# Retention: where a head's decay logarithms and exponentials stand in the order of VectorE and ScalarE

## The chip, the cores and the metric

One core of a Trainium2 chip runs one program: two layers of a first block (retention, windowed attention, feed-forward) and one layer of a second block. The metric is the device time of one execution in microseconds; lower is better. The engines are TensorE (PE in the profile, its weight loads PEld), VectorE (DVE), ScalarE (ACT), GpSimd (POOL) and SyncE (SP). Each has its own instruction queue and works it off strictly in order; they meet only at semaphores.

## What is computed

The change touches only the retention branch of the two layers of the first block. There are 8 heads, head width 64 for q and k and 128 for v, over 528 positions (16 meta tokens and 512 others). The reference works in chunks:

```
decay_in = jnp.where(mask[None], jnp.exp(lg * jnp.maximum(rel, 0.0)[None]), 0.0)
s = jnp.einsum('bhncd,bhnkd->bhnck', q, k) * decay_in[:, None]
o_in = jnp.einsum('bhnck,bhnke->bhnce', s, v)
...
mu = jnp.mean(o, axis=-1, keepdims=True)
var = jnp.mean(jnp.square(o - mu), axis=-1, keepdims=True)
o = (o - mu) * lax.rsqrt(var + EPS)
return o * jax.nn.silu(gate)
```

with a forward direction and a backward one, each with its own decay per head. The kernel uses the closed form without chunks: for one head, out = (scores times decay) times v over all positions, where the decay of a pair of positions is the exponential of min(a·rel, b·rel), rel being their distance with its sign, a and b the two directions' logarithmic decays. Then comes a normalisation over the 128 columns of v, and the product with silu of the gate.

## The kernel before

The kernel is written by hand for each engine: for each stage a function for PE, ACT, DVE and POOL, whose Python loops print that engine's queue. Nothing reorders afterwards. `wait_ge` waits on a semaphore of another engine, `tick` names the event that an instruction signals.

The retention stage is `ret_pe`, `ret_act`, `ret_dve`, `ret_pool`, run once in each of the two layers (l = 0 and 1). In layer 0 a tile is 528 wide, in layer 1 it is 512 wide. All four loop over h = 0 to 9 and hold a software pipeline: a turn h works on the scores of head h, on the mean of head h-1 and on the variance, scale and gate of head h-2. A "turn" below is one such pass.

- PE, turn h: five score tiles, j = 0 to 4 (L192, inputs QK; tile 0 has 16 rows, the others 128, the contraction is over 64 rows); the gate projection of head h-2, called g below (L302 to L304); five products with v, called ret (L198), each of which needs its decayed score tile; the variance of h-2 and the mean of h-1 (L192, inputs WK, MH).
- DVE, turn h: two instructions that make the 128x928 table of logarithms DT[h % 2] (L623 and L625, "logs"); five multiplications of a score tile in PSUM by a window of the table (L635, "decay"); the low half of a coming weight tile (L270); the scaling of head h-2 (L643, "normed"); the subtraction of the mean of head h-1 (L647, "dev").
- ACT, turn h: the exponential of the table in place (L587, "decays"); the high half of a coming weight tile (L260); silu of g (L593); the copy of ret out of PSUM (L598, "o"); Ln and Exp that make the reciprocal deviation of head h-2 (L348, L351); the square of head h-1 (L607). ACT loads a function table ahead of silu, of Ln and of Exp (ACT_TABLE_LOAD).
- POOL, turn h: the product of head h-2 with silu (L658).

Each PE tile takes the next of four pairs of PSUM banks in a ring (`ps.take`), and waits until the tile that had it four takes before has been read (`ps.give`). There are nine takes in a full turn, so from the order of the takes: score 1 waits for the copy "o" of the turn before, score 2 for Ln of the turn before, score 3 for "dev" of the turn before (L647 on DVE), score 4 for the first decay multiplication of this turn (L635, j = 0), and g for the second one.

The two tables DT[0] and DT[1] are both in use before and after; head h uses DT[h % 2]. The six decayed score tiles are a ring too.

Of the kernel before, what the change touches and what calls it, by code (L numbers as in the profile page):

```python
# [84 lines left out]
def program(nc, A, out, known, seen):  # L85
    F, U32, FR = mybir.dt.float32, mybir.dt.uint32, mybir.dt.float32r
    ALU, ACT, AX = mybir.AluOpType, mybir.ActivationFunctionType, mybir.AxisListType
# [3 lines left out]
    with ctx:  # L91
# [35 lines left out]
        def sem(name):  # L127
            return ctx.enter_context(nc.semaphore(name))

        T, V, S, G = (Progress(n, sem(n), known, seen) for n in ("pe_done", "dve_done", "act_done", "pool_done"))  # L130
# [14 lines left out]
        def stage_end(q, tag):  # L145
            q.mark("end", tag)

        def after_all(e, tag):
            for q in (T, V, S, G):
                e.wait_ge(q.sem, q.at("end", tag))  # L150
# [28 lines left out]
        def pv(b, n, rows=128):  # L179
            return PSM[0:rows, b:b + 2, 0:264] if n == TT else PSM[0:rows, b, 0:n]  # L180

        def fv(ap, n):
            return ap.rearrange("p (a b) -> p a b", a=2) if n == TT else ap
# [162 lines left out]
        def rstd_act(e, tag, n, rs, scale, *done):  # L346
            e.wait_ge(T.sem, T.at(done[0], tag, *done[1:]))
            e.activation(fv(rs[:, 0:n], n), pv(ps.of("ss", tag), n), ACT.Ln, bias=eps, scale=scale).then_inc(S.sem, S.tick())  # L348
            ps.give(S, "ss", tag)
            e.wait_ge(S.sem, S.n)  # L350
            e.activation(rs[:, 0:n], rs[:, 0:n], ACT.Exp, scale=-0.5).then_inc(S.sem, S.tick("rstd", tag))  # L351
# [31 lines left out]
        DT = [WK[:, oX + i * 928:oX + i * 928 + 928] for i in range(2)]  # L383
# [146 lines left out]
        def lg(l, d, h):  # L530
            c = oVec + 80 + 16 * l + 8 * d + h
            return MH[:, c:c + 1]
# [44 lines left out]
        def ret_act(e, l):  # L577
            n = TT - 16 * l
            after_all(e, ("in", l))
            if l == 0:  # L580
                all_ = MH[:, oVec + 80:oVec + 112]
                e.wait_ge(con_in, 64)
                e.activation(all_, all_, ACT.Exp).then_inc(S.sem, S.tick("lg"))
            for h in range(10):
                if h < 8:
                    e.wait_ge(V.sem, V.at("logs", l, h))
                    e.activation(DT[h % 2], DT[h % 2], ACT.Exp).then_inc(S.sem, S.tick("decays", l, h))  # L587
                if h >= 2:
                    W.act(e, first["fill", l] + h - 2 + 3)
                    e.wait_ge(T.sem, T.at("g", l, h - 2))  # L590
                    if h >= 4:
                        e.wait_ge(G.sem, G.at("gated", l, h - 4))
                    e.activation(fv(gx[h % 2][:, 0:n], n), pv(ps.of("g", l, h - 2), n), ACT.Silu).then_inc(  # L593
                        S.sem, S.tick("g", l, h - 2))
                    ps.give(S, "g", l, h - 2)
                if h < 8:
                    e.wait_ge(T.sem, T.at("ret", l, h, 4))
                    e.activation(fv(oS[h][:, 0:n], n), pv(ps.of("ret", l, h), n), ACT.Copy).then_inc(  # L598
                        S.sem, S.tick("o", l, h))
                    ps.give(S, "ret", l, h)  # L600
                if h >= 2:
                    rstd_act(e, ("ret", l, h - 2), n, sq2[h % 2], 1.0, "var")
                if 1 <= h < 9:
                    e.wait_ge(V.sem, V.at("dev", l, h - 1))
                    if h >= 3:
                        e.wait_ge(V.sem, V.at("normed", l, h - 3))
                    e.activation(sq2[(h - 1) % 2][:, 0:n], oS[h - 1][:, 0:n], ACT.Square).then_inc(S.sem, S.tick("dev2", l, h - 1))  # L607
            stage_end(S, ("ret", l))

        def ret_dve(e, l):  # L610
            c0 = 16 * l
            n = TT - c0
            after_all(e, ("in", l))
            if l == 0:
                e.wait_ge(S.sem, S.at("lg"))
                for i in (0, 2):
                    ap = MH[:, oVec + 80 + 8 * i:oVec + 88 + 8 * i]
                    e.tensor_scalar(ap, ap, -1.0, None, MUL).then_inc(V.sem, V.tick())
            for h in range(10):
                if h < 8:  # L620
                    dt = DT[h % 2]
                    e.wait_ge(V.sem, V.n)
                    e.tensor_scalar(dt, con["rel"], lg(l, 0, h), None, MUL).then_inc(V.sem, V.tick())  # L623
                    e.wait_ge(V.sem, V.n)
                    e.scalar_tensor_tensor(out=dt, in0=con["rel"], scalar=lg(l, 1, h), in1=dt, op0=MUL,  # L625
                                           op1=MIN).then_inc(V.sem, V.tick("logs", l, h))
                    for j, (j0, nj) in enumerate(JT):
                        e.wait_ge(T.sem, T.at("score", l, h, j))
                        if j == 0:
                            e.wait_ge(S.sem, S.at("decays", l, h))  # L630
                        i = 5 * h + j
                        if i >= 6:
                            e.wait_ge(T.sem, T.at("ret", l, (i - 6) // 5, (i - 6) % 5))
                        win = dt[0:nj, c0 - j0 + 400:c0 - j0 + 400 + n]
                        e.scalar_tensor_tensor(out=fv(sd[i % 6][0:nj, 0:n], n), in0=pv(ps.of("score", l, h, j), n, nj),  # L635
                                               scalar=0.125, in1=fv(win, n), op0=MUL, op1=MUL).then_inc(
                                                   V.sem, V.tick("decay", l, h, j))
                        ps.give(V, "score", l, h, j)
                if h >= 2:
                    W.dve(e, first["fill", l] + h - 2 + 3)  # L640
                    o = oS[h - 2]
                    e.wait_ge(S.sem, S.at("rstd", ("ret", l, h - 2)))
                    e.tensor_tensor(o[:, 0:n], o[:, 0:n], sq2[h % 2][:, 0:n], MUL).then_inc(V.sem, V.tick("normed", l, h - 2))  # L643
                if 1 <= h < 9:
                    o = oS[h - 1]
                    e.wait_ge(T.sem, T.at("mean", l, h - 1))
                    e.scalar_tensor_tensor(out=fv(o[:, 0:n], n), in0=pv(ps.of("mean", l, h - 1), n), scalar=-1.0,  # L647
                                           in1=fv(o[:, 0:n], n), op0=MUL, op1=ADD).then_inc(V.sem, V.tick("dev", l, h - 1))
                    ps.give(V, "mean", l, h - 1)
            stage_end(V, ("ret", l))  # L650
# [1953 lines left out]
        with nc.Block() as block:  # L2604
# [14 lines left out]
            @block.vector  # L2619
            def vector(e):  # L2620
                for l in range(2):
                    in_dve(e, l)
                    ret_dve(e, l)
                    att_dve(e, l)
                    mix_dve(e, l)
                    ff_dve(e, l)
                mxp_dve(e)
                gdn_dve(e)
                mxo_dve(e)
                xa_dve(e)  # L2630
                peer_dve(e)

            @block.scalar
            def scalar(e):
                e.dma_start(MH[:, oS_:oS_ + C_S], A["consts"][:, 0:C_S]).then_inc(con_in, 16)
                e.dma_start(MH[:, oVec:oVec + 112], A["vec1"]).then_inc(con_in, 16)
                e.dma_start(CN[:, :], A["consts"][:, C_S:]).then_inc(con_in, 16)
                e.dma_start(MH[:, oVec2:oVec2 + 129], A["vec2"]).then_inc(con_in, 16)
                for l in range(2):
                    in_act(e, l)  # L2640
                    ret_act(e, l)
                    att_act(e, l)
                    mix_act(e, l)
                    ff_act(e, l)
                mxp_act(e)
                gdn_act(e)
                mxo_act(e)
                xa_act(e)
                peer_act(e)
# [174 lines left out]
```

## Time and profile before

| | us |
|---|---|
| median of 3 runs | 4329.08 |
| lowest, highest | 4317.47, 4329.37 |
| profiled execution, own time | 4314.43 |
| its span (first to last instruction) | 4312.6 |

The trace gives each instruction's start and length on its engine. In a timeline a row is: start, duration, engine, line, operation, output<-input, shapes, count, and in brackets the idle time before the row and the instruction that ended it. Rows that follow each other without a gap are merged and counted. A matmul's length contains its tail after the next has begun, so the speed of a PE stretch is read from start to start. In a table of windows a row is a stretch, its length, then for PE, PEld, DVE, ACT and POOL the busy time with the number of instructions, then the granted PE clock (1.00 is 2.4 GHz, 0.50 is 1.2 GHz), the DMA share and GB/s.

### The profile page before, as it was taken

The numbers are of one execution on the slowest core, as the hardware profiler recorded it, in microseconds if no ns is written. First come the engines' busy times: TensorE is split into PE (matmuls) and PEld (weight loads), VectorE is DVE, ScalarE is ACT, GpSimd is POOL, SyncE is SP. The second block draws the span as 40 slices with busy tenths as digits, with TensorE's granted clock in tenths as the row PEclk, the third lists the DMA queues.
The fourth block names the chain that finished last, engine by engine and source line by source line (L and its number), as shares of the span: only waits on it lengthen the run. The fifth ranks groups of instructions, "written<-read, shape, count | busy, mean of one in ns | idle before, by whom it ended". The sixth has DMA issues, their size and how long they took to land.

```text
span 4312.6 us, 55249 instructions
## 1 busy us (share of the span) xinstructions
PE 4029.1 (93%) x22280; PEld 3477.1 (81%) x22280; DVE 2153.1 (50%) x3812; ACT 1462.2 (34%) x2104; POOL 739.8 (17%) x721
## 2 busy tenths in 40 slices
PE   7988997999798899799979988899999999999998
PEld 6967797999694467588857887589999888999997
DVE  3333444434433344443446543327996665566664
ACT  3133333222323433322236443333333333333332
POOL 1000000110000000011001340005765662111100
PEclk9988998999898899999989999999999999999999
DMA  3101121222120111222212112135765668888873
GB/s 117 60 25 39 46 74 49 94 89 92 51 74 30 34 48 66 70 94 92 95 48 83 40 50 93 49 93 166 228 205 186 217 220 271 287 266 263 266 249 124
DMA packets 229132, 511.00 MB, mean 118 GB/s; under 512 B 35792, under 2 KB 134224, under 8 KB 228368
## 3 DMA queue, kind: packets, MB, share of 16 engines
q1 hardware_dynamic: 190432, 404.87, 29.8%
q0 software_dynamic: 18432, 67.12, 4.5%
q10 hardware_dynamic: 20016, 35.48, 2.2%
q8 instruction: 178, 2.92, 0.3%
q14 instruction: 74, 0.61, 0.0%
HBM read 446.27 MB, written 60.82 MB: 118 GB/s over the span
## 4 chain that ended last, share of the span: by engine, by line
PE 85%; DVE 7%; ACT 4%; issue 2%; DMA 1%; SPq 1%; POOL 0%; ACTq 0%; DVEq 0%; POOLq 0%
PE PSM L302 18%; PE PSM L303 17%; PE PSM L304 17%; PE PSM L192 5%; PE PSM L2292 5%; PE PSM L2294 5%; PE PSM L2293 5%; PE PSM L198 4%; PE PSM L2268 2%; PE PSM L692 1%; DMA RAW<-peer_u_dram 1%; PE PSM L724 1%; DVE UX L329 1%; PE PSM L1670 1%; ACT L348 1%
## 5 line engine op out<-in xcount | busy, mean ns | idle before, releaser
L302 PE MATMUL PSM<-UX,PARTS 128*128 128x264 f32 (+2 forms) x3424 | 1217.9, 356 | 50.6 <-DVE UX L329 29.7
L303 PE MATMUL PSM<-UX,PARTS 128*128 128x264 f32 (+2 forms) x3424 | 1193.9, 349 | 0.0
L304 PE MATMUL PSM<-UX,PARTS 128*128 128x264 f32 (+2 forms) x3424 | 1189.1, 347 | 0.0
L270 DVE TENSOR_TENSOR PARTS<-RAW,PARTS 128x1024 fp32r<-128x1024 f32 x533 | 652.2, 1229 | 624.5 <-ACT PARTS L260 624.4
L260 ACT ACTIVATE PARTS<-RAW 128x1024 fp32r<-128x1024 f32 x596 | 626.8, 1054 | 890.1 <-PE PSM L2294 415.1
L302 PEld LDWEIGHTS PSM<-UX,PARTS 128*128 128x128 f32 x3424 | 659.5, 193 | 149.9 <-DVE UX L329 41.7
L303 PEld LDWEIGHTS PSM<-UX,PARTS 128*128 128x128 f32 x3424 | 660.1, 193 | 65.0 <-issue 4.3
L304 PEld LDWEIGHTS PSM<-UX,PARTS 128*128 128x128 f32 x3424 | 658.4, 192 | 64.0
L2292 PE MATMUL PSM<-AC,PARTS 128*128 128x448 f32 x1024 | 375.3, 366 | 2.5 <-DVE AC L2534 2.5
L2294 PE MATMUL PSM<-AC,PARTS 128*128 128x448 f32 x1024 | 374.6, 366 | 0.0
L2293 PE MATMUL PSM<-AC,PARTS 128*128 128x448 f32 x1024 | 374.6, 366 | 0.0
L304 PE MATMUL PSM<-HD,PARTS 128*128 128x264 f32 (+1 forms) x768 | 247.7, 322 | 0.0
L303 PE MATMUL PSM<-HD,PARTS 128*128 128x264 f32 (+1 forms) x768 | 245.5, 320 | 0.0
L302 PE MATMUL PSM<-HD,PARTS 128*128 128x264 f32 (+1 forms) x768 | 245.3, 319 | 0.0
L277 POOL TENSOR_TENSOR PARTS<-RAW,PARTS 128x1024 fp32r<-128x1024 f32 x63 | 163.6, 2598 | 439.8 <-ACT PARTS L260 439.7
L2292 PEld LDWEIGHTS PSM<-AC,PARTS 128*128 128x128 f32 x1024 | 192.8, 188 | 18.0 <-ACT AC L2375 2.9
L2294 PEld LDWEIGHTS PSM<-AC,PARTS 128*128 128x128 f32 x1024 | 192.7, 188 | 15.3
L2293 PEld LDWEIGHTS PSM<-AC,PARTS 128*128 128x128 f32 x1024 | 192.8, 188 | 15.2
L2573 POOL TENSOR_SCALAR MQ<-MH,MQ 128x128 f32<-128x128 f32 x224 | 187.0, 850 | 63.9 <-PE PSM L2268 45.5
L1073 POOL TENSOR_TENSOR FT<-FT 128x528 f32<-128x528 f32 (+1 forms) x64 | 67.5, 1054 | 746.7 <-ACT FT L1052 746.7
L1087 DVE TENSOR_TENSOR HD<-FT,HD 128x528 fp32r<-128x528 f32 (+1 forms) x64 | 65.2, 1019 | 252.8 <-ACT HD L1039 252.8
L2340 ACT ACTIVATE MQ<-PSM 128x448 f32<-128x448 f32 x128 | 69.4, 543 | 350.4 <-PE PSM L304 350.4
(357 smaller groups left out, 5519.5 us busy)
## 6 DMA issues: line engine op xcount, KB each, us to landing
RAW<-w_ff_dram SPq DMA_DIRECT2D x128, 512.0 KB, 3.4
RAW<-peer_u_dram SPq DMA_DIRECT2D x128, 512.0 KB, 4.0
RAW<-peer_v_dram SPq DMA_DIRECT2D x128, 512.0 KB, 4.5
RAW<-w_in_dram SPq DMA_DIRECT2D x116, 512.0 KB, 3.5
acts_dram<-MQ ACTq DMA_DIRECT2D x128, 224.0 KB, 4.1
MQ<-acts_dram SPq DMA_DIRECT2D x128, 224.0 KB, 3.6
MQ<-gates_dram SPq DMA_DIRECT2D x128, 224.0 KB, 4.4
gates_dram<-MQ SPq DMA_DIRECT2D x48, 512.0 KB, 8.4
```

The costliest lines, as they stand in the source:

```text
L192: m = e.matmul(PSM[0:rows, b + s, 0:hi - lo], lhs[k], rhs[k][:, lo:hi], start=(k == 0), stop=(k == len(lhs) - 1))
L198: m = e.matmul(PSM[:, b + s, 0:hi - lo], lhs, rhs[:, lo:hi], start=(k == 0), stop=(k == of - 1), skip_group_check=True)
L260: e.activation(p[:, 0:1024], self.raw.of(i), ACT.Copy).then_inc(S.sem, S.tick("w", i))
L270: e.tensor_tensor(p[:, 1024:2048], self.raw.of(i), p[:, 0:1024].bitcast(F), SUB).then_inc(V.sem, V.tick("w", i))
L277: e.tensor_tensor(p[:, 1024:2048], self.raw.of(i), p[:, 0:1024].bitcast(F), SUB).then_inc(G.sem, G.tick("w", i))
L302: e.matmul(dst, wh[k], xh_[k][:, lo:hi], start=(k == 0), stop=False, skip_group_check=True)
L303: e.matmul(dst, wh[k], xl_[k][:, lo:hi], start=False, stop=False, skip_group_check=True)
L304: m = e.matmul(dst, wl[k], xh_[k][:, lo:hi], start=False, stop=(k == kk - 1), skip_group_check=True)
L2292: e.matmul(PSM[:, acc[d], 0:TD], vh[d], ah, start=(i == 0), stop=False, skip_group_check=True)
L2293: e.matmul(PSM[:, acc[d], 0:TD], vh[d], al, start=False, stop=False, skip_group_check=True)
L2294: m = e.matmul(PSM[:, acc[d], 0:TD], vl[d], ah, start=False, stop=(i == NB - 1), skip_group_check=True)
L2573: e.tensor_scalar(o[:, 128 * i:128 * i + 128], iota, E2[:, t0 + i:t0 + i + 1], None, ALU.is_equal).then_inc(G.sem, G.tick("onB", i4))
```

## The change

In `ret_dve` the two logs instructions become a function `logs(h)`. It is called for head 0 ahead of the loop, for head 1 at the beginning of turn 0, and from turn 1 on for head h+1 behind the five decay multiplications of turn h. In `ret_act` the exponential of the table is made for heads 0 and 1 at the beginning of turn 0, and then for head h+1 at the beginning of turn h. Nothing else differs: no tile, buffer, shape or number of instructions, and nothing on PE, POOL or SP.

```
@@ ret_act
             for h in range(10):
-                if h < 8:
-                    e.wait_ge(V.sem, V.at("logs", l, h))
-                    e.activation(DT[h % 2], DT[h % 2], ACT.Exp).then_inc(S.sem, S.tick("decays", l, h))
+                for n_ in (0, 1) if h == 0 else (h + 1,):
+                    if n_ < 8:
+                        e.wait_ge(V.sem, V.at("logs", l, n_))
+                        e.activation(DT[n_ % 2], DT[n_ % 2], ACT.Exp).then_inc(S.sem, S.tick("decays", l, n_))
@@ ret_dve
-            for h in range(10):
+            def logs(h):
+
                 if h < 8:
                     dt = DT[h % 2]
...
+
+            logs(0)
+            for h in range(10):
+                if h == 0:
+                    logs(1)
+                if h < 8:
+                    dt = DT[h % 2]
                     for j, (j0, nj) in enumerate(JT):
...
                         ps.give(V, "score", l, h, j)
+                    if h >= 1:
+                        logs(h + 1)
```

The first place is DVE at the start of the stage in layer 0: L623 and L625 are the logs (L625 and L627 in the new file), L635 the decay multiplications (L644), L647 the dev of head 0 (L658). Before:

```order
L623 TENSOR_SCALAR WK<-CN,MH 128x928
L625 SCALAR_TENSOR_TENSOR WK<-CN,MH,WK 128x928
L635 SCALAR_TENSOR_TENSOR WK<-PSM,WK 16x528
L635 SCALAR_TENSOR_TENSOR WK<-PSM,WK 128x528 x4
L623 TENSOR_SCALAR WK<-CN,MH 128x928
L625 SCALAR_TENSOR_TENSOR WK<-CN,MH,WK 128x928
L635 SCALAR_TENSOR_TENSOR WK<-PSM,WK 16x528
L635 SCALAR_TENSOR_TENSOR WK<-PSM,WK 128x528 x4
L647 SCALAR_TENSOR_TENSOR WK<-PSM,WK 128x528
```

The same place on DVE now:

```order
L625 TENSOR_SCALAR WK<-CN,MH 128x928
L627 SCALAR_TENSOR_TENSOR WK<-CN,MH,WK 128x928
L625 TENSOR_SCALAR WK<-CN,MH 128x928
L627 SCALAR_TENSOR_TENSOR WK<-CN,MH,WK 128x928
L644 SCALAR_TENSOR_TENSOR WK<-PSM,WK 16x528
L644 SCALAR_TENSOR_TENSOR WK<-PSM,WK 128x528 x4
L644 SCALAR_TENSOR_TENSOR WK<-PSM,WK 16x528
L644 SCALAR_TENSOR_TENSOR WK<-PSM,WK 128x528 x4
L625 TENSOR_SCALAR WK<-CN,MH 128x928
L627 SCALAR_TENSOR_TENSOR WK<-CN,MH,WK 128x928
L658 SCALAR_TENSOR_TENSOR WK<-PSM,WK 128x528
```

The logs of head 1 have moved ahead of the decay multiplications of head 0, and those of head 2 ahead of the dev of head 0.

The second place is DVE from the end of turn 2 to the end of turn 3 (L270 is a weight's low half, L643 normed, L654 in the new file). Before:

```order
L643 TENSOR_TENSOR WK<-WK 128x528
L647 SCALAR_TENSOR_TENSOR WK<-PSM,WK 128x528
L623 TENSOR_SCALAR WK<-CN,MH 128x928
L625 SCALAR_TENSOR_TENSOR WK<-CN,MH,WK 128x928
L635 SCALAR_TENSOR_TENSOR WK<-PSM,WK 16x528
L635 SCALAR_TENSOR_TENSOR WK<-PSM,WK 128x528 x4
L270 TENSOR_TENSOR PARTS<-RAW,PARTS 128x1024
```

The same place on DVE now:

```order
L654 TENSOR_TENSOR WK<-WK 128x528
L658 SCALAR_TENSOR_TENSOR WK<-PSM,WK 128x528
L644 SCALAR_TENSOR_TENSOR WK<-PSM,WK 16x528
L644 SCALAR_TENSOR_TENSOR WK<-PSM,WK 128x528 x4
L625 TENSOR_SCALAR WK<-CN,MH 128x928
L627 SCALAR_TENSOR_TENSOR WK<-CN,MH,WK 128x928
L270 TENSOR_TENSOR PARTS<-RAW,PARTS 128x1024
```

The decay multiplications of head 3 now follow the dev of head 2 at once, and the logs stand behind them, for head 4. On ACT, whose rows read alike in both from turn 1 on, the exponential (L587, L588 in the new file) stays between the square (L607) and the weight's high half (L260), but is that of the next head; at the start of the stage the two exponentials of heads 0 and 1 stand together, where before the copy "o" of head 0 lay between them.

## Rows read from the trace of the kernel before

**Rows 1.** Page: the chain that ended last, by engine.

```profile
PE 85%; DVE 7%; ACT 4%; issue 2%; DMA 1%; SPq 1%; POOL 0%; ACTq 0%; DVEq 0%; POOLq 0%
```

**Rows 2.** Windows: the two retention stages, to the last full turn.

```profile
197.75:376.00 178.25, 155.25 (x764) 123.48 (x764) 63.44 (x81) 66.10 (x76) 8.95 (x7) 0.88 0.07 24
1306.40:1482.00 175.60, 151.25 (x388) 73.46 (x388) 63.42 (x80) 67.90 (x77) 8.92 (x7) 0.88 0.07 24
```

**Rows 3.** Timeline of PE, layer 0, turns 2, 3 and 5.

```profile
223.24 1.15 PE L192 MATMUL PSM<-QK 64*128 64x264 f32 x4 [0.70 <-DVE WK L635]
224.33 0.39 PE L302 MATMUL PSM<-UX,PARTS 128*128 128x264 f32 x1
...
230.32 4.91 PE L198 MATMUL PSM<-WK,QK 16*128 16x264 f32 x20
...
236.94 3.04 PE L192 MATMUL PSM<-QK 64*16 64x264 f32 x12
241.26 1.15 PE L192 MATMUL PSM<-QK 64*128 64x264 f32 x4 [1.28 <-DVE WK L647]
245.63 2.12 PE L192 MATMUL PSM<-QK 64*128 64x264 f32 x4 [3.22 <-DVE WK L635]
247.68 0.59 PE L302 MATMUL PSM<-UX,PARTS 128*128 128x264 f32 x1
...
254.79 4.91 PE L198 MATMUL PSM<-WK,QK 16*128 16x264 f32 x20
...
291.45 2.13 PE L192 MATMUL PSM<-QK 64*128 64x264 f32 x4 [1.28 <-DVE WK L647]
```

**Rows 4.** Timeline of DVE, layer 0, from the dev of turn 2.

```profile
240.50 0.70 DVE L647 SCALAR_TENSOR_TENSOR WK<-PSM,WK 128x528 f32<-128x528 f32 x1
241.24 1.32 DVE L623 TENSOR_SCALAR WK<-CN,MH 128x928 f32<-128x928 f32 x1
242.59 1.18 DVE L625 SCALAR_TENSOR_TENSOR WK<-CN,MH,WK 128x928 f32<-128x928 f32 x1
244.88 2.54 DVE L635 SCALAR_TENSOR_TENSOR WK<-PSM,WK 16x528 f32<-16x528 f32 x4 [1.10 <-ACT WK L587]
```

**Rows 5.** Timeline of ACT, layer 0, turn 3.

```profile
243.81 0.98 ACT L587 ACTIVATE WK<-WK 128x928 f32<-128x928 f32 x1 [1.94 <-DVE WK L625]
...
259.74 0.61 ACT L598 ACTIVATE WK<-PSM 128x528 f32<-128x528 f32 x1 [4.23 <-PE PSM L198]
...
263.67 0.64 ACT L351 ACTIVATE WK<-WK 128x528 f32<-128x528 f32 x1
```

**Rows 6.** Timeline of DVE: dev of turn 7, layer 0; turns 2 and 7, layer 1.

```profile
365.79 0.70 DVE L647 SCALAR_TENSOR_TENSOR WK<-PSM,WK 128x528 f32<-128x528 f32 x1
...
1349.26 0.68 DVE L647 SCALAR_TENSOR_TENSOR WK<-PSM,WK 128x512 f32<-128x512 f32 x1
...
1469.36 0.68 DVE L647 SCALAR_TENSOR_TENSOR WK<-PSM,WK 128x512 f32<-128x512 f32 x1
```

**Rows 7.** Timeline of PE, layer 1: score 4 of turns 2 and 3.

```profile
1332.48 1.12 PE L192 MATMUL PSM<-QK 64*128 64x512 f32 x2 [0.79 <-DVE WK L635]
...
1354.33 2.07 PE L192 MATMUL PSM<-QK 64*128 64x512 f32 x2 [2.26 <-DVE WK L635]
```

**Rows 8.** Windows: three stretches of low PE clock.

```profile
318.00:325.50 7.50, 4.80 (x17) 3.91 (x18) 5.23 (x7) 3.21 (x3) 0.00 (x0) 0.54 0.00 1
342.00:352.50 10.50, 7.33 (x28) 6.45 (x29) 5.66 (x8) 3.21 (x3) 0.00 (x0) 0.51 0.16 50
1321.50:1325.50 4.00, 4.00 (x6) 1.65 (x6) 0.00 (x0) 0.00 (x0) 0.00 (x0) 0.57 0.00 0
```

**Rows 9.** Timeline of PE, layer 1: ret of heads 0 and 1.

```profile
1311.39 4.75 PE L198 MATMUL PSM<-WK,QK 16*128 16x512 f32 x10
...
1320.66 6.45 PE L198 MATMUL PSM<-WK,QK 16*128 16x512 f32 x10
```

**Rows 10.** Timeline of DVE, layer 0: first decay multiplications, logs of head 1.

```profile
201.47 3.15 DVE L635 SCALAR_TENSOR_TENSOR WK<-PSM,WK 16x528 f32<-16x528 f32 x5 [1.12 <-ACT WK L587]
204.66 0.70 DVE L623 TENSOR_SCALAR WK<-CN,MH 128x928 f32<-128x928 f32 x1
```

## The prediction

> **What bounds the kernel now.** I read first the chain that ended last: PE carries 85% of it, DVE 7%, ACT 4% [rows 1], so a DVE or ACT instruction costs time only where PE stands still for it. Second, the windows of the two retention stages: 178.25 and 175.60 us, PE busy for 155.25 and 151.25, so it idles some 47 us in them and its clock averages 0.88 [rows 2]. The reader is to see that these stages, 8% of the span, leave PE idle and slowed down although 85% of the chain is PE.
>
> Third, PE's timeline of one turn, for what ends its waits [rows 3]. Turn 3 of layer 0: three score tiles from 236.94; 1.28 us idle until L647 (dev) has freed the bank for score 3, at 241.26; 3.22 us idle until L635 (the first decay multiplication) has freed the bank for score 4, at 245.63; g from 247.68; ret from 254.79. DVE's timeline says why the second wait is there [rows 4]: dev ends at 240.50 + 0.70 = 241.20, then come the logs, 1.32 and 1.18, then 1.10 of idling until ACT's exponential, 0.98 [rows 5], and only at 244.88 the first decay multiplication, 3.68 us after dev. The scores 0 to 2 of this head had been in PSUM all along. Nothing in the table of logarithms depends on the scores: it is late only by its place.
>
> The turn's loop is closed through ACT: ret ends, its copy starts at 259.74, Exp of the deviation ends at 263.67 + 0.64 = 264.31 [rows 5], normed and dev follow, and the next turn's score 3 may start. So the path of one turn is: dev, logs, exponential, decay multiplication, score 4, g, ret, copy, Ln, Exp, normed, dev. I call the end of dev t0 and count turns from t0 to t0.
>
> **The turn before, in parts.** From score 4 to the next t0: in turn 2 of layer 0 PE ran at the full clock, 223.24 to 241.20 = 17.96 us [rows 3, 4]; in layer 1, 1332.48 to 1349.94 = 17.46 [rows 6, 7]. From t0 to score 4: 241.20 to 245.63 = 4.43 in layer 0, 1349.94 to 1354.33 = 4.39 in layer 1 [rows 3, 4, 6, 7]. So a turn without loss of clock would take 22.39 and 21.85. The five turns 3 to 7 took, from 241.20 to 366.49, 125.29 us in layer 0 (25.06 each), and from 1349.94 to 1470.04, 120.10 in layer 1 (24.02 each) [rows 4, 6]. The difference, 2.67 and 2.17 a turn, is the low clock: score 4 of turn 3 lasts 2.12 instead of 1.15, and g 7.11 (247.68 to 254.79) instead of 5.99 (224.33 to 230.32) [rows 3].
>
> **What the change does to a turn.** In turns 3 to 7 the decay multiplications follow dev at once. DVE frees score 4's bank about 0.7 us after t0, while PE is still in score 3, which takes from start to start what score 4 takes in turn 2, 1.09 us (223.24 to 224.33) [rows 3]. So score 4 starts at t0 + 0.06 + 1.09, where 0.06 is dev's end to score 3 (241.20 to 241.26), and the turn without loss of clock is 0.06 + 1.09 + 17.96 = 19.11 in layer 0; in layer 1, where I take 0.06 + 1.06, it is 18.58. Removed per turn: 3.28 and 3.27.
>
> What hides the moved work: DVE does five multiplications (3.15 for five [rows 10]) and then logs, which end at about t0 + 5.5; ACT's exponential ends at t0 + 6.5. They are needed a turn later, at t0 + 19. Behind the exponential on ACT's queue stand the weight copy (1.04), the table load (1.28), silu, and the copy of ret. By their durations silu ends near t0 + 9.5, and ret ends near t0 + 13.1 (1.15 + 5.99 + the 4.91 of ret, plus score 4): over 3 us of slack before the path would notice. DVE's weight half (L270) comes near t0 + 9, and normed is wanted only at t0 + 17.7. The weight is for a tile three turns on, so neither PE nor SP's load waits for it. If that cover were gone, each microsecond of ACT's lateness would be a microsecond of the turn. No table load is added: the exponential still stands behind another Exp. L623 took 1.32 where GpSimd's product overlapped it and 0.70 elsewhere [rows 4, 10]; that gain is off the path and counts nothing.
>
> **The start of a stage.** The logs of head 1 now stand ahead of the first multiplication, 0.70 + 1.18 + gaps = 1.93, in place of the 1.12 that DVE idled there for the exponential [rows 4, 10]: +0.81. Head 1 gains nothing, as PE never waited there. In turn 2 the 0.70 (layer 1: 0.79) that PE idled for L635 goes [rows 3, 7]. Net +0.11 and +0.02.
>
> **The clock, which decides the size.** The low clock does not come from the second wait alone. In turn 5 score 3 already took 2.13 directly after an idle of only 1.28 [rows 3], a wait that the change leaves in place. In layer 1 the clock was 0.57 over 4.00 us in which PE was busy for all of them, and ret of head 1 took 6.45 instead of 4.75 [rows 8, 9]: 1.70 lost with no idle at all, behind a long run of score tiles. So with the 3.2 us wait gone, the turn still holds 1.28 of idle among five score tiles, and I expect the clock to fall in most turns. Its price then has two ends. Below: nothing. Above: before, a low stretch was 7.5 to 10.5 us with PE busy for 4.80 and 7.33 of it [rows 8]; PE idles little there now, so a stretch of 7 us would cost up to 3.4 to 3.5. I take 1.70, the price seen when PE was busy throughout, the nearest row to what the turn becomes.
>
> The Trainium skill, page "TensorE: Matmul & The Clock Gate", part 1, says that half rate follows idleness and full rate sustained activity, and in "Loop structure matters more than you think" that back-to-back matmuls keep the array at full rate. By that rule the new turn would lose nothing (rival A). The fall with PE busy throughout speaks against it.
>
> **Sum.** Layer 0: 5 x (19.11 + 1.70) = 104.05 against 125.29, a gain of 21.24. Layer 1: 5 x (18.58 + 1.70) = 101.40 against 120.10, a gain of 18.70. Less 0.11 and 0.02: **39.8 us**. On the profiled execution's 4314.43 that gives 4274.6, on the median 4329.08 it gives 4289.3. The four times of this kernel lie in two pairs, 4314 and 4317, 4329 and 4329, so I count from 4325, between their mean (4322.6) and the median: **4285**.
>
> **Rivals.**
> A. The clock stays up. For it: turn 2 kept it, with its 0.70 wait [rows 3]. Against: the two falls above. Gain 5 x (25.06 - 19.11) + 5 x (24.02 - 18.58) - 0.1 = 56.8, so 4268.
> B. The clock's price doubles to 3.4 a turn, because low stretches keep their length while PE has work all through them. Gain 5 x (25.06 - 22.51) + 5 x (24.02 - 21.98) - 0.1 = 22.8, so 4302.
> C. The change does not do what it says: the freed 3.3 us turn into another wait in the same turn, such as ACT reaching the copy of ret late. For it: ACT's queue now waits some 2.7 us longer at the head of the turn. Against: the 3 us of slack. About 4325, no change.
> D. Slower. The low clock lasts until the end of g in every turn, as PE, released early, runs the scores and the beginning of g slowly. Then score 3, score 4 and g cost 2.1 + 6.0 = 8.1 more a turn, 5 x (8.1 - 5.95) + 5 x (8.1 - 5.44) + 0.1 = 24 us slower, 4349. It decides from 5.95 (layer 0) and 5.44 (layer 1) of loss a turn on. Against: the largest mean loss seen is 2.67, and the low stretches ended inside g.
>
> **Chances.** Forecast, gains of 30 to 50: 0.62. A, over 50: 0.17. B, 13 to 30: 0.13. C: 0.05. D: 0.03. What a measurement of this kernel can tell from no change is about 0.3%, 13 us; so faster 0.92, same 0.05, slower 0.03. The range reaches from A counted from the profiled execution (4258) to short of C: 4259 to 4308.
>
> **What would show it.** In the changed profile: L644 starts within 0.1 us of the end of L658; PE's wait for L644 ahead of score 4 is gone, the wait for L658 ahead of score 3 (1.28) remains; turns 3 to 7 take 19 to 22.5 us; the PE clock still dips once in most turns; L588 starts some 5 us after t0, and the copy L599 right at the end of ret. It would be wrong if ACT idled before the exponential so long that L599 came late (C), if the turns were all at 19.1 (A), or if g took 10 us or more throughout (D). The rest of the kernel should only shift.

## The result, and the profile after

| | before | after |
|---|---|---|
| median, us | 4323.28 | 4287.79 |
| lowest to highest | 4317.47 to 4329.37 | 4281.48 to 4293.43 |
| profiled execution | 4314.43 | 4289.13 |

The ratio is 0.9917, 95% interval 0.9894 to 0.9941. A second comparison gave 0.9927, 0.9913 to 0.9941, medians 4320.86 and 4290.35. The forecast was 4285 (4259 to 4308) with a gain of 39.8 us; the medians differ by 35.5 and 30.5 us. The two profiled executions differ by only 25.3 us, and the section on the repeated profiles shows why that is too little.

The page of the changed kernel, chain by engine, and the windows of its two retention stages (stretch, length, busy time of PE, PEld, DVE, ACT and POOL, clock, DMA); they answer to [rows 1, 2]:

```profile
PE 86%; DVE 6%; ACT 3%; DMA 2%; issue 2%; POOL 0%; SPq 0%; ACTq 0%; DVEq 0%; POOLq 0%
```

```profile
197.35:355.00 157.65, 149.94 (x763) 121.85 (x764) 60.52 (x81) 65.65 (x74) 8.29 (x7) 0.92 0.08 27
1285.13:1446.00 160.87, 152.11 (x388) 75.27 (x388) 60.83 (x80) 67.58 (x76) 8.93 (x7) 0.89 0.08 26
```

PE's idle in them has fallen from 47 us to 16.5, while its clock has risen only from 0.88 to 0.92 and 0.89. One turn of the changed kernel, turn 4 of layer 0, on PE, DVE and ACT, in that order (L658 is dev, L644 the decay multiplications, L625 and L627 the logs, L588 their exponential, L599 the copy of ret); it answers to [rows 3 to 5]:

```profile
264.45 2.13 PE L192 MATMUL PSM<-QK 64*128 64x264 f32 x8 [1.28 <-DVE WK L658]
266.52 0.59 PE L302 MATMUL PSM<-UX,PARTS 128*128 128x264 f32 x1
...
273.96 4.91 PE L198 MATMUL PSM<-WK,QK 16*128 16x264 f32 x20
```

```profile
263.70 0.70 DVE L658 SCALAR_TENSOR_TENSOR WK<-PSM,WK 128x528 f32<-128x528 f32 x1
264.31 3.14 DVE L644 SCALAR_TENSOR_TENSOR WK<-PSM,WK 16x528 f32<-16x528 f32 x5
267.50 0.70 DVE L625 TENSOR_SCALAR WK<-CN,MH 128x928 f32<-128x928 f32 x1
268.23 1.19 DVE L627 SCALAR_TENSOR_TENSOR WK<-CN,MH,WK 128x928 f32<-128x928 f32 x1
...
284.15 0.70 DVE L658 SCALAR_TENSOR_TENSOR WK<-PSM,WK 128x528 f32<-128x528 f32 x1
```

```profile
269.45 0.98 ACT L588 ACTIVATE WK<-WK 128x928 f32<-128x928 f32 x1 [4.38 <-DVE WK L627]
270.34 1.04 ACT L260 ACTIVATE PARTS<-RAW 128x1024 fp32r<-128x1024 f32 x1
271.40 1.28 ACT L594 ACT_TABLE_LOAD   x1
274.07 0.61 ACT L594 ACTIVATE WK<-PSM 128x528 f32<-128x528 f32 x1 [1.39 <-PE PSM L304]
278.91 0.61 ACT L599 ACTIVATE WK<-PSM 128x528 f32<-128x528 f32 x1 [4.23 <-PE PSM L198]
```

The wait of 3.2 us ahead of score 4 is gone: scores 3 and 4 run as one row of eight instructions. The wait of 1.28 for dev stands as before. The multiplications follow dev at once, L588 starts 5.05 us after dev's end at 264.40, and ACT still idles 1.39 + 4.23 us before it is needed. The turn is 284.85 - 264.40 = 20.45 us. But g takes 273.96 - 266.52 = 7.44 where the full clock gives 5.99 [rows 3]. The clock in that stage of the changed kernel, in windows of the next turn and of turn 3 in layer 1:

```profile
286.50:290.50 4.00, 4.00 (x20) 3.60 (x19) 3.29 (x5) 0.60 (x1) 0.00 (x0) 0.57 0.02 4
...
1331.00:1338.50 7.50, 7.50 (x18) 4.90 (x17) 5.10 (x7) 3.21 (x3) 0.00 (x0) 0.54 0.00 0
```

PE is busy for the whole of both, and near 1.2 GHz. Read from the ends of dev, the turns 3 to 7 are:

| us | before | predicted | after |
|---|---|---|---|
| layer 0, five turns | 125.29 | 104.05 | 103.87 |
| layer 1, five turns | 120.10 | 101.40 | 104.58 |
| turn 2, layers 0 and 1 | 21.76, 21.25 | 0.70 and 0.79 less | 20.81, 20.22 |
| first score to dev of turn 1, layer 0 | 21.69 | 0.81 more | 24.12 |
| the same, layer 1 | 22.29 | 0.81 more | 24.57 |

### The profile page after: what moved, and what is told of

The parts are those of the page before. It is cut to its first block, busy times and chain, and to the rows that moved or that the text cites. A ratio compares the mean times of both kernels' runs of the same rounds, so it can differ in the third digit from the quotient of the medians.

```text
span 4287.3 us, 55249 instructions
## 1 busy us (share of the span) xinstructions
PE 4030.1 (94%) x22280; PEld 3471.3 (81%) x22280; DVE 2143.4 (50%) x3812; ACT 1462.6 (34%) x2104; POOL 741.2 (17%) x721
## 4 chain that ended last, share of the span: by engine, by line
PE 86%; DVE 6%; ACT 3%; DMA 2%; issue 2%; POOL 0%; SPq 0%; ACTq 0%; DVEq 0%; POOLq 0%
PE PSM L302 18%; PE PSM L303 17%; PE PSM L304 17%; PE PSM L192 6%; PE PSM L2303 5%; PE PSM L2305 5%; PE PSM L2304 5%; PE PSM L198 4%; PE PSM L2279 2%; DMA RAW<-peer_u_dram 1%; PE PSM L703 1%; PE PSM L735 1%; DVE UX L329 1%; PE PSM L1681 1%; PE PSM L1668 1%
## 5 line engine op out<-in xcount | busy, mean ns | idle before, releaser
L270 DVE TENSOR_TENSOR PARTS<-RAW,PARTS 128x1024 fp32r<-128x1024 f32 x533 | 652.2, 1230 | 658.5 <-ACT PARTS L260 607.0
L260 ACT ACTIVATE PARTS<-RAW 128x1024 fp32r<-128x1024 f32 x596 | 626.8, 1054 | 904.2 <-PE PSM L2305 426.9
```

Of the source, the lines that this page charges most:

```text
L260: e.activation(p[:, 0:1024], self.raw.of(i), ACT.Copy).then_inc(S.sem, S.tick("w", i))
L270: e.tensor_tensor(p[:, 1024:2048], self.raw.of(i), p[:, 0:1024].bitcast(F), SUB).then_inc(V.sem, V.tick("w", i))
```

## The experiments

"Turns" below are turns 3 to 7, each from the end of dev to the end of the next dev. Each edit is one to the changed kernel (the last of the kernel edits one to the reordered kernel), and the turns are compared with those of the changed kernel; the ratios are to the kernel before. The turns of an experiment come from one profiled execution.

### The logarithms early, the exponential in its old place

```diff
-                for n_ in (0, 1) if h == 0 else (h + 1,):
-                    if n_ < 8:
-                        e.wait_ge(V.sem, V.at("logs", l, n_))
-                        e.activation(DT[n_ % 2], DT[n_ % 2], ACT.Exp).then_inc(S.sem, S.tick("decays", l, n_))
+                if h < 8:
+                    e.wait_ge(V.sem, V.at("logs", l, h))
+                    e.activation(DT[h % 2], DT[h % 2], ACT.Exp).then_inc(S.sem, S.tick("decays", l, h))
```

> Half of the change: DVE's logarithms are made a head ahead as in the changed kernel, ACT's exponential stays at the head of its own turn as before. My theory (the path from dev to score 4 is what counted, and every piece of it counts alone): after dev come ACT's square (0.64) and exponential (0.98), so the first decay multiplication starts about 1.7 us after dev instead of 3.68 (before) or 0 (changed); score 4 waits some 1.3 us; a turn without loss of clock is 0.7 + 1.7 + 17.96 + 0.1 = 20.5 us (before 22.4, changed 19.1), with the clock's loss 22 to 23.5. In time 16 to 22 us under before. Rival (the exponential had been the last to come and the logs were hidden behind something else): no gain, turns of 25 us.

Measured: ratio to before 0.9959 (0.9943 to 0.9974), median 4301.23 against 4317.06. The profiled execution was the slowest of the five (4313.76). Its turns sum to 116.59 and 113.84, 23.3 and 22.8 each. ACT and DVE of this kernel after one dev (L657; L607 the square, L587 the exponential, L643 the multiplications):

```profile
288.31 0.64 ACT L607 ACTIVATE WK<-WK 128x528 f32<-128x528 f32 x1 [1.39 <-DVE WK L657]
288.86 0.96 ACT L587 ACTIVATE WK<-WK 128x928 f32<-128x928 f32 x1
```

```profile
287.58 0.70 DVE L657 SCALAR_TENSOR_TENSOR WK<-PSM,WK 128x528 f32<-128x528 f32 x1
289.91 2.54 DVE L643 SCALAR_TENSOR_TENSOR WK<-PSM,WK 16x528 f32<-16x528 f32 x4 [1.63 <-PE PSM L192]
```

Dev ends at 288.28 and the multiplications start 1.63 later, behind the square and the exponential, as worked out (1.7). The wait is put down to PE there; by the times it is the exponential, which ends at 289.82. PE's score 4 then follows:

```profile
290.66 2.12 PE L192 MATMUL PSM<-QK 64*128 64x264 f32 x4 [1.17 <-DVE WK L643]
```

From dev to score 4 it is 2.38 us, where before it was 4.43 and after the change 1.15 is left for score 3: of 3.28 us that the whole change takes out of the path, the logs alone take 2.05. Of these 2.05 the turns show 1.5 (245.39 to 230.43 for ten). In layer 0 a turn without loss would be 2.38 + 17.96 = 20.3, so the clock now takes 3.0 a turn, where it took 2.67. Each piece of the path counts by itself, and a part of each goes to the clock.

### The start of the stage as before

```diff
             for h in range(10):
-                if h == 0:
-                    logs(1)
...
-                    if h >= 1:
-                        logs(h + 1)
+                    logs(h + 1)
```

> The changed kernel, but the logs of head 1 stand behind the decay multiplications of head 0 on DVE, as before; ACT as in the changed kernel. Theory: the start of the stage costs 0.8 of delay and, when it lengthens PE's idle from 0.5 to 1.3 us, a fall of the clock in ret of head 0 (6.60 instead of 4.91, and 7.60 instead of 4.75 in layer 1). So dev of turn 1 should come 2.4 us earlier in layer 0 and 2 to 2.5 us earlier in layer 1, 4 to 5 us in all, turns 3 to 7 unchanged at 20 to 22 us. Rival (the clock falls in ret of head 0 or 1 anyway, as it did in layer 1 of the kernel before with PE busy): 1.6 us in all.

Measured: median 4281.87, ratio to before 0.9912 (0.9890 to 0.9934). From the first score to dev of turn 1 it takes 21.68 us in layer 0 and 20.59 in layer 1, that is 2.44 and 3.98 less than in the changed kernel; in layer 1 up to 2.5 had been expected. PE at the start of layer 0, first in the changed kernel and then in this one:

```profile
202.56 1.16 PE L192 MATMUL PSM<-QK 64*128 64x264 f32 x4 [1.29 <-DVE WK L644]
203.65 6.60 PE L198 MATMUL PSM<-WK,QK 16*128 16x264 f32 x20
```

```profile
201.81 1.15 PE L192 MATMUL PSM<-QK 64*128 64x264 f32 x4 [0.54 <-DVE WK L642]
202.89 4.91 PE L198 MATMUL PSM<-WK,QK 16*128 16x264 f32 x20
```

The wait grows by 0.75, as the forecast said, but ret of head 0 also takes 1.69 longer, at the low clock. That second part the forecast left out. It can't be put down to the longer wait alone: in two other profiles of the kernel before, ret of head 0 took 6.60 and 6.56 with the short wait of 0.54. In all five profiles of the changed kernel it took 6.60 to 8.65. Of the turns, those of layer 0 stay (103.70), and those of layer 1 come to 101.10 instead of 104.58. The order of instructions in these turns is the same; the four turns of layer 1 that took 21.5 to 21.6 now take 19.94 to 19.97, and the one that took 18.38 takes 21.30. So it is the clock again, with its falls at other points; what sets these is open.

### PE's wait for dev filled with work

```diff
                         for q, v in back:
                             e.wait_ge(q.sem, v)
+                        if j == 2 and h >= 3:
+                            gemm(e, b, [con["onesm"]], [con["cosR"][:, 0:n]], n)
                         gemm(e, b, [k_], [q_], n, rows=nj).then_inc(T.sem, T.tick("score", l, h, j))
```

> The changed kernel with work added: in turns 3 to 7, ahead of score 2, PE multiplies a constant 128x128 by a constant 128x528 (or 512) into the bank that score 2 then overwrites; 0.97 us a turn at the full clock, inside the 1.28 us in which PE waits for dev. Nothing else is changed. Theory (the rest of the turn's length over 19.1 and 18.6 is the clock falling around that wait): if the wait is what brings the clock down, turns 3 to 7 take 19.1 and 18.6 us, 13 to 20 us less in all than the changed kernel. Rival (the clock falls in the stretch of score tiles whether PE idles or not, as in ret of head 1 before): turns stay at 20.4 to 21.6, and the time is that of the changed kernel, or up to 1 us a turn longer.

Measured: median 4262.01, ratio to before 0.9863 (0.9835 to 0.9892), though PE does more work. The turns are 18.91 to 18.93 in layer 0 and 18.37 to 18.40 in layer 1. Two rows of PE's timeline, the filler and the scores 2 to 4 behind it, and a window a little longer than a turn:

```profile
299.10 1.16 PE L192 MATMUL PSM<-CN,MH 128*128 128x264 f32 x4
300.19 3.20 PE L192 MATMUL PSM<-QK 64*128 64x264 f32 x12
```

```profile
284.00:303.00 19.00, 19.00 (x102) 14.79 (x101) 7.58 (x11) 8.98 (x10) 1.31 (x1) 1.00 0.08 29
```

The clock stays at 2.4 GHz and the turn is 0.2 shorter than the 19.11 and 18.58 that the forecast gave for a turn without loss. If the filled turn is taken for the turn without loss, the price of the clock in the changed kernel is 103.87 - 94.59 = 9.3 us in layer 0 and 104.58 - 91.92 = 12.7 in layer 1, 1.86 and 2.53 a turn, where 1.70 was taken. The filler does two things, it ends the idle and it adds matmuls of full height among scores that use 64 rows; the run does not tell which of them holds the clock.

### PE's turn reordered: score 0, g, scores 1 to 4

```diff
@@ ret_pe, in the loop over j, behind the score's gemm
+                        if j == 0 and h >= 2:
+                            g_tile(h)
@@ ret_act
-                    W.act(e, first["fill", l] + h - 2 + 3)
...
+                if h >= 2:
+                    W.act(e, first["fill", l] + h - 2 + 3)
...
@@ ret_dve
-                if h == 0:
-                    logs(1)
...
-                    if h >= 1:
-                        logs(h + 1)
+                        if j == (0 if h >= 2 else 4):
+                            logs(h + 1)
```

> The changed kernel with PE's turn reordered: score 0, g, scores 1 to 4, ret; ACT makes silu ahead of the exponential (one more table load a turn), and DVE makes the next logs behind the first decay multiplication. The 6 us of g then lie where PE waited 1.28 us for dev. Theory: no wait of PE is left in turns 3 to 7, and a turn is the sum of PE's work, 2 x 0.97 + 4.8 + 5.9 + 4.8 = 17.6 us (layer 1: 17.1), if the clock holds; 1.5 to 3 us a turn less than the changed kernel, 20 to 35 us in all, plus what the clock gives. Rival (ACT's longer queue takes over: the copy of ret waits for the weight copy): turns of 19 us or more with PE idle ahead of score 1 or g. Second rival: the clock falls in the scores anyway, and a turn is 19 to 20 us.

Measured: median 4240.52, ratio to before 0.9812 (0.9792 to 0.9832). The turns are 17.37 and 16.75 us, all ten within 0.04 of these. PE of one turn, from score 0 on; g lies in the gap between the first two rows:

```profile
271.26 1.06 PE L192 MATMUL PSM<-QK 64*16 64x264 f32 x4
...
278.26 3.82 PE L192 MATMUL PSM<-QK 64*128 64x264 f32 x16
282.01 4.91 PE L198 MATMUL PSM<-WK,QK 16*128 16x264 f32 x20
286.76 1.94 PE L192 MATMUL PSM<-WK,MH 128*128 128x264 f32 x8
288.63 1.06 PE L192 MATMUL PSM<-QK 64*16 64x264 f32 x4
```

No row has a wait. This version beats both kernels; it keeps all the work and adds one table load a turn on ACT. It also makes the logs of head 1 behind the multiplications of head 0, as the second experiment does, so its median contains that difference too; its turns don't.

### ACT's queue made longer

```diff
+                if 3 <= h < 8:
+                    for _ in range(16):
+                        e.wait_ge(S.sem, S.n)
+                        e.activation(WK[:, 11360:11696], con["cosR"][:, 0:336], ACT.Copy).then_inc(S.sem, S.tick())
                 if h >= 2:
                     W.act(e, first["fill", l] + h - 2 + 3)
```

> The changed kernel with work added on ACT: in turns 3 to 7, between the exponential and the weight copy, 16 copies of a constant 128x336 into an unused part of a buffer, each waiting for the one before, some 0.5 us each, 8 us a turn. In the changed kernel's trace ACT idles 1.39 us ahead of silu and 4.23 us ahead of the copy of ret, 5.6 in all. Theory (that idle is the cover of the moved exponential): the first 5.6 us are hidden and the rest lengthens the turn, 20.4 to about 23 us, 10 turns, 25 us in all. If the cover is only the 3 us of the prediction: 25.5 us a turn. If ACT's queue was on the path all along: 28 to 29 us a turn.

Measured: one execution, 4307.35; four turns of layer 0 take 24.60, the others 21.8 to 24.4, 23.9 in the mean of all ten; by the number expected (23) a miss. ACT of this kernel in one turn (L592 the added copies, L598 silu, L603 the copy of ret), then DVE of the same turn (L662 dev):

```profile
273.04 0.98 ACT L588 ACTIVATE WK<-WK 128x928 f32<-128x928 f32 x1 [6.00 <-DVE WK L631]
274.05 8.21 ACT L592 ACTIVATE WK<-CN 128x336 f32<-128x336 f32 x16
...
285.03 0.60 ACT L603 ACTIVATE WK<-PSM 128x528 f32<-128x528 f32 x1
```

```profile
265.66 0.70 DVE L662 SCALAR_TENSOR_TENSOR WK<-PSM,WK 128x528 f32<-128x528 f32 x1
```

The copy of ret has no wait left, so ACT is now the bound from the exponential to this copy. Its exponential starts 6.68 us after dev (266.36) instead of 5.05, since scores 3 and 4 ran at the low clock and the logs came later. 20.45 + 8.21 - 5.62 of idle + 1.63 = 24.67, against 24.60. The cover of the moved exponential is thus the idle that the trace shows, 5.6 us, not the 3 us of the forecast; it was never in danger.

### The first two tables a stage earlier, in the reordered kernel

```diff
@@ in_dve
             for t in range(1, 5):
+                if t == 4:
...
+                    logs_(e, l, 0)
+                    logs_(e, l, 1)
                 tok(t)
@@ in_act, behind tok(3)
+                    for n_ in (0, 1):
+                        e.wait_ge(V.sem, V.at("logs", l, n_))
+                        e.activation(DT[n_], DT[n_], ACT.Exp).then_inc(S.sem, S.tick("decays", l, n_))
```

> The reordered kernel (score 0, g, scores 1 to 4, ret), and the logs and exponentials of heads 0 and 1 are made in the stage before, ahead of its last tile's copies. Theory: PE no longer waits for the first decay multiplication at the start of retention (1.3 us) and the clock does not fall in ret of head 0 (1.7 and 2.8 us): from the start of the stage to dev of turn 1 some 3 to 5 us less in each layer, 6 to 10 us in all against the reordered kernel, 4231 to 4235. Rival (the four instructions ahead of the copies hold up the last tile of the stage before, which PE waits for): gained at one place and lost at the other, within 3 us.

Measured: median 4241.21, against 4240.52 of the reordered kernel: no gain, where 6 to 10 us had been expected. From the first score to dev of turn 1 it takes 20.87 instead of 23.37 in layer 0, but in layer 1 only 20.19 instead of 20.59, since there the clock had not fallen in the reordered kernel's execution. One turn of layer 1 then took 18.46 instead of 16.75. In turns 3 to 7 PE had not waited once, and its clock had been 1.00 for 73 us (first row); then it fell in ret of that turn (second row), which took 6.45 instead of 4.75:

```profile
1304.50:1377.50 73.00, 73.00 (x212) 36.91 (x210) 33.34 (x44) 44.27 (x48) 6.04 (x5) 1.00 0.09 29
1377.60:1381.60 4.00, 4.00 (x7) 1.69 (x7) 1.82 (x2) 0.00 (x0) 0.00 (x0) 0.65 0.23 60
```

The rival's other half, a loss in the stage before, is not seen: PE waits 0.52 ahead of the first score of layer 0 in both, and from the last dev of layer 0 to the first score of layer 1 they take the same to 0.2 us. The 2.9 us of gain at the start are below what these times can tell; whether they are real in the mean stays open.

### Repeated profiles, for the pace of the last loop

The changed kernel's execution was ahead of the kernel before by 38.5 us at the last MAX8 of the second block (3170.3 against 3208.8), and only by 25.5 at the end of its last loop (L2534, L2545 in the new file). The question was whether the change does that.

> The changed kernel again, for a tighter ratio and a second profile. Theory (PE's pace in the last loop, with its matmuls of 448 columns, is a property of the execution, 202.7 or 206.7 ns a matmul, not of the kernel): the median stays near 4287, the single times spread over some 12 us, and the profile may show either pace. Turns 3 to 7 sum to about 104 us in layer 0 and 100 to 105 in layer 1. Rival (the change has brought the slower pace of that loop): the slower pace again, and no time below 4280.

> The kernel before again, one look. Theory (as above): the retention turns sum to 125 and 120 us again within 2 us, as the clock's falls allow; the last loop shows 611 or 623 us from its first to its last product on VectorE, either of them. Rival (the pace belongs to the kernel): 611 again.

> The changed kernel again, one look, for the pace of the last loop (611 us from its first to its last product on VectorE at 202.7 ns a matmul, 623 at 206.7). So far the kernel before showed 611 twice, the changed kernel 623 twice, variants of it 611 twice and 623 four times. Theory (a property of the execution): one of three more looks at the changed kernel shows 611, with a time of 4275 to 4283. Rival (a property of the changed program): 623 three times more.

> As the run before it: the changed kernel, one look, 611 or 623 in the last loop. By either theory the retention turns 3 to 7 sum to 102 to 105 us in each layer.

> As the two before it: the changed kernel, one look. By the theory of the execution at least one of the three has the fast pace, by that of the program none.

> The kernel before, one look. Its times so far lie at 4314 to 4321 and at 4324 to 4332. Theory (the execution): with about a third of chance 623 us in the last loop and a time over 4325, else 611 and a time under 4322. Rival (the program): 611.

The product on VectorE of that loop, from its first to its last start: the first profile of before, the third of before, the first of after, and the third of after.

```profile
L2534 DVE TENSOR_TENSOR AC<-MQ,AC x128: 615/618/626, 3661.5 to 4272.8; 128x448 fp32r<-128x448 f32 x128
```

```profile
L2534 DVE TENSOR_TENSOR AC<-MQ,AC x128: 615/616/626, 3665.2 to 4288.4; 128x448 fp32r<-128x448 f32 x128
```

```profile
L2545 DVE TENSOR_TENSOR AC<-MQ,AC x128: 615/617/625, 3624.1 to 4247.3; 128x448 fp32r<-128x448 f32 x128
```

```profile
L2545 DVE TENSOR_TENSOR AC<-MQ,AC x128: 615/618/626, 3624.2 to 4235.4; 128x448 fp32r<-128x448 f32 x128
```

Both kernels show both lengths, 611 and 623 us, so neither pace belongs to one of the programs. Whether the change makes one of them more frequent, one of three against two of five can't tell. Sorted by the pace, the executions that have a profile are:

| | last loop 610 to 611 us | last loop 623 us |
|---|---|---|
| before | 4314.43, 4323.94 | 4330.26 |
| after | 4276.99, 4280.71, 4281.38 | 4289.13, 4290.94 |
| difference of means | 39.5 | 40.2 |

Like against like, the change is worth some 40 us, and at the last MAX8, ahead of that loop, the mean of the five profiles after lies 39.8 us before the mean of the three before. The medians give 30 to 36; that this comes from a mix of the two paces is likely, but most of those executions have no profile. With so few executions that figure is good to some 5 us: the kernel before alone spreads by 9.5 at one pace. The retention turns hold meanwhile: 103.76 to 103.91 in layer 0 in all five profiles of the changed kernel, 102.8 to 104.6 in layer 1; 125.3 to 125.9 and 120.1 to 122.1 before.

## Why the prediction was right, step by step

**The wait.** Right, and shown by halves: the logs alone shorten the way from dev to score 4 by 2.05 us, with the exponential it is 3.28. The wait removed was 3.3 us a turn in both layers.

**The turn without loss of clock.** 19.11 and 18.58 were forecast; the filled kernel shows 18.92 and 18.38. The difference is small: scores 3 and 4 together take 1.97 there (301.35 to 303.32), while the forecast counted twice the 1.09 of a score that stood alone.

**The clock.** Right in kind: it falls in nearly every turn although the long wait is gone, so rival A (56.8 us) did not come. Its price was mis-sized: 1.70 a turn was taken, 1.86 and 2.53 are measured. In layer 0 the turns came to the forecast's number only because the two errors, 0.2 a turn too much work and 0.16 too little loss, cancel. In layer 1 they do not, and the gain there was 15.5 us instead of 18.7. Single turns lost 3.2 (21.59 against 18.38), near rival B's 3.4, but the mean did not, and one turn of layer 1 lost nothing (18.38, under the 19 to 22.5 that were to be seen).

**The start of a stage.** This step failed in size: +0.81 a layer was forecast, +2.43 and +2.28 measured in the first profiles, +2.9 and +2.1 in the means of three profiles before and five after. The delay itself was right; the forecast priced the lengthened idle as idle alone and forgot there what it had said of the turns, that the clock may fall after it. In the first profile that costs 1.69 us in ret of head 0 in layer 0, and in layer 1 2.85, against 1.70 lost in ret of head 1 before [rows 9]. Turn 2 was to give back 0.70 and 0.79 and gave 0.95 and 1.03.

**The cover on ACT.** Right, and larger than said: 5.6 us of idle, not over 3, because ret ends 1.4 us later than reckoned (t0 + 14.5 instead of 13.1), as g is slow at the low clock, and the exponential ends 0.5 earlier (t0 + 6.0 instead of 6.5).

**Rivals C and D.** Neither came. No new wait took the place of the old one: the copy L599 starts as ret ends, and the largest turn after is 22.13 us, less than any of turns 3 to 7 before.

**The rest.** Summed over the two stages the first profile gives 36.9 us from the turns and 2.0 from turn 2, less 4.7 at the starts: 34.2. By the last MAX8 it is 38.5. The other 4 us arise where the change does nothing: 3.0 between the second retention stage and that MAX8, 0.9 between the two retention stages, 0.4 ahead of the first. No run took this apart. In the means of three and five profiles it is alike: 38.4 from the turns, 2.5 from turn 2, less 5.0, so 35.9 of the 39.8. The forecast's 39.8 was meant for the two stages alone and was some 4 us too high for them; that the whole kernel gained 40 is luck.

## What to carry to other kernels

A table that depends on nothing in the loop belongs ahead of the loop's critical hand-over, and what it gains is the length of the path that it leaves. Here that was 3.28 us, of the 3.68 between the two DVE instructions that it stood between. Before counting a removed wait in full, look at what the clock does in the turn that is left: with a wait of 1.3 us among the score tiles, 1.9 to 2.5 us a turn went to slow matmuls, more than the wait itself. Other PE work put into that wait paid: 22 us in the turns for useless work, 38 us for g itself.

## What the runs showed of the hardware that was not expected

- PE's clock can be near 1.2 GHz over a stretch in which PE never idles: 0.57 over 4.00 us and 0.54 over 7.50 us, each shortly after a run of 64-row score tiles with a wait of 1.3 us. The same tiles with the wait filled, or with g between them, keep 1.00 in all ten turns. A wait is not needed for a fall, though: with g between them and PE never idle, it fell once in ten turns of the run with the first two tables early, after 73 us at 1.00. What brings it down is open.
- The Trainium skill, page "TensorE: Matmul & The Clock Gate", part 1, has the clock follow activity. The filled kernel agrees: more PE work, 22 us less in its turns. The half rate after idleness, which the prediction draws from the same part, does not cover the falls above with PE busy. By it the new turn would have lost nothing, and it lost 1.86 and 2.53 us: the measurement decides.
- The turns settle: in layer 0 of the changed kernel four turns in a row take 20.42 to 20.45, and in its other four profiles 20.43 to 20.49.
- In the last loop (3072 matmuls of 448 columns at a clock of 1.00) one execution has 202.7 ns from start to start and another 206.7, evenly through the loop, 12 us in all. What sets it is open.
